# Seven half-size block products in place of eight in the first projection of a squared-ReLU MLP, from the second chunk on

## The reference, cut to what matters

```python
x = x + y
x = x + squared_relu_mlp(rms_norm(x, mlp_norm[i]), mlp_w1[i], mlp_w2[i])
```

## Time and profile before

| what | value |
| --- | --- |
| median of 3 runs | 2267.03 us (2266.93 to 2268.66) |
| the profiled execution | 2264.53 us |
| its span in the profile | 2262.7 us (1.8 us lie around it) |
| TensorE busy | 2093.1 us, 93% of the span |
| VectorE, ScalarE, GpSimd busy | 1262.4, 968.8 and 260.1 us |
| the MLP | about 1594 to 2259 us of the span |

### The profile page before, as it was taken

The page is one execution under the profiler, slowest core; times in us unless marked ns, Lnnn a source line. Parts: engine busy times, 40 slices in busy tenths (PEclk is TensorE's granted clock), DMA queues, the critical chain, the costliest instruction groups (busy, mean ns, idle before and its releaser), DMA issues. The chain is left out here.

```text
span 2262.7 us, 28831 instructions
## 1 busy us (share of the span) xinstructions
PE 2093.1 (93%) x11131; PEld 1095.9 (48%) x11131; DVE 1262.4 (56%) x1346; ACT 968.8 (43%) x1256; POOL 260.1 (11%) x263
## 2 busy tenths in 40 slices
PE   7988988889499999999958999969899999999999
PEld 5445446644354454454435665624444444444444
DVE  5134237743799999999976352555443333433432
ACT  5122226722388888888845342452311211211210
POOL 0000130000133333333200000050000000000000
PEclk9999999999699999999979999989999999999999
DMA  6111220051399999999984352342220111111101
GB/s 265 38 38 38 71 51 1 1 217 47 109 416 412 412 404 410 399 400 404 367 310 156 104 187 62 92 126 108 75 75 37 38 73 37 62 49 37 37 0 75
DMA packets 74718, 352.98 MB, mean 156 GB/s; under 512 B 16336, under 2 KB 23120, under 8 KB 42064
## 3 DMA queue, kind: packets, MB, share of 16 engines
q1 hardware_dynamic: 56304, 305.21, 34.7%
q0 software_dynamic: 18336, 46.69, 6.3%
HBM read 326.67 MB, written 29.36 MB: 157 GB/s over the span
## 5 line engine op out<-in xcount | busy, mean ns | idle before, releaser
L409 PE MATMUL ps<-xt,split 128*128 128x512 f16 (+1 forms) x1024 | 377.8, 369 | 10.0 <-issue 8.3
L410 PE MATMUL ps<-xt,split 128*128 128x512 f16 (+1 forms) x1024 | 378.0, 369 | 0.0
L411 PE MATMUL ps<-xt,split 128*128 128x512 f16 (+1 forms) x1024 | 377.9, 369 | 0.0
L409 PE MATMUL ps<-split,xt 128*128 128x512 f16 x928 | 354.0, 381 | 25.5 <-DMA xt<-arena 19.5
L410 PE MATMUL ps<-split,xt 128*128 128x512 f16 x928 | 353.9, 381 | 0.0
L411 PE MATMUL ps<-split,xt 128*128 128x512 f16 x928 | 353.6, 381 | 0.0
L540 DVE SCALAR_TENSOR_TENSOR split<-stage,split 128x2048 f16<-128x2048 f32 x128 | 289.4, 2282 | 5.6 <-ACT split L536 3.9
L536 ACT ACTIVATE split<-stage 128x2048 f16<-128x2048 f32 x128 | 240.5, 1904 | 94.2 <-PE ps L411 94.2
L1773 DVE SCALAR_TENSOR_TENSOR resid<-ps,resid 128x512 f32<-128x512 f32 x128 | 87.1, 690 | 191.7 <-PE ps L411 191.6
L409 PE MATMUL ps<-split,arena 128*128 128x512 f16 x512 | 194.0, 379 | 0.0
L410 PE MATMUL ps<-split,arena 128*128 128x512 f16 x512 | 194.0, 379 | 0.0
(11 more groups left out here) (293 smaller groups left out, 3149.4 us busy)
## 6 DMA issues: line engine op xcount, KB each, us to landing
stage<-in_w_gate SPq DMA_DIRECT2D x64, 1024.0 KB, 7.4
stage<-in_w_up SPq DMA_DIRECT2D x64, 1024.0 KB, 7.7
arena<-in_w_down SPq DMA_DIRECT2D x64, 1024.0 KB, 8.3
stage<-in_w_mlp SPq DMA_DIRECT2D x32, 1024.0 KB, 5.0
arena<-in_conv_taps POOLq DMA_DIRECT2D x32, 576.0 KB, 4.2
stage<-in_w_dense_a SPq DMA_DIRECT2D x16, 1024.0 KB, 7.7
stage<-in_w_dense_b SPq DMA_DIRECT2D x12, 1024.0 KB, 9.6
resid<-in_x SPq DMA_DIRECT2D x16, 512.0 KB, 4.8
```

The costliest lines, as they stand in the source:

```text
L409: nc.tensor.matmul(out_ap, lh, rh, start=start, stop=False)
L410: nc.tensor.matmul(out_ap, lh, rl, start=False, stop=False)
L411: return nc.tensor.matmul(out_ap, ll, rh, start=False, stop=stop)
```

## The change

It replaces the first projection of chunks 1 to 7. A chunk's w1 is cut into four quarters, A11, A21 (slot 0) and A12, A22 (slot 1); the first index is the half of the features, the second the half of the inputs in the order that the loads bring them. The input is cut into four blocks by input half and token half. Eight products of a quarter with a block become seven (Strassen's scheme in the form with S1 to S4 on the weight side, T1 to T4 on the input side).

- **TensorE:** seven products (`PRODUCTS`), each two groups (f = 0 into `PS`, f = 1 into `PT`) of 4 pieces x 3 = 12 matmuls of 512 columns.
- **GpSimd:** in each chunk, four sums of 128x1024 float32 in place in `stage` (S1, S3, S2, S4), after the low part of A22 has been made.
- **ScalarE, VectorE:** seven operands of 128x1024 are split (`op_hi`, `op_lo`) instead of two units of 128x2048.
- **Once, in chunk 0:** VectorE makes T1 to T4, in two parts each, from `XT2` (`combo_of`, 20 operations of 128x1024, every one with two operands in SBUF), then their low parts (`combo_lo`, 8); ScalarE makes the high parts (`combo_hi`, 8). T1 comes in the second projection of chunk 0.
- **VectorE, in each chunk from 1 on:** 14 sums of products (`bank_sum`, 128x512), 8 relu-times-itself (`quad_relu`) and 8 low parts (`quad_lo`); ScalarE 2 copies and 8 high parts.
- **SP:** slots 0 and 1 are reloaded once all seven operands of the chunk have been split (`s_pl`).
- w1 is laid out by quarters in DRAM. A few semaphores of earlier stages are shared; their counts are raised to match.

```diff
         def mlp_chunks(eng, body):
-            with eng.Fori(0, NC - 1) as c:
+            with eng.Fori(1, NC - 1) as c:
                 body(c, False)
             body(NC - 1, True)
...
+        OP_AT = {"A11": split[:, 0:2048], "A12": split[:, 2048:4096], "S4": split[:, 4096:6144],
+                 "A22": split[:, 6144:8192], "S2": Z[:, 0:1024].bitcast(F16), "S3": junk[:, :].bitcast(F16),
+                 "S1": Z[:, 1280:2304].bitcast(F16)}
...
+        PRODUCTS = ["A11", "A12", "S2", "S3", "A22", "S1", "S4"]
...
+        FACTOR = {"A11": "B11", "A12": "B21", "S4": "B22", "A22": "T4", "S1": "T1", "S2": "T2", "S3": "T3"}
+        COMBOS = [("T3", 0), ("T3", 1), ("T2", 0), ("T2", 1), ("T4", 0), ("T4", 1), ("T1", 0), ("T1", 1)]
...
                 for s in range(SLOTS):
-                    sp.wait_ge(s_wh[s], RM + c)
-                    sp.wait_ge(s_wo[s], RM + c)
+                    if s < 2 and not (isinstance(c, int) and c < 2):
+                        sp.wait_ge(s_pl, 7 * (c - 1))
+                    else:
+                        sp.wait_ge(s_wh[s], RM + c)
+                        sp.wait_ge(s_wo[s], RM + c)
...
+            with pool.Fori(1, NC) as c:
+                for s in range(2):
+                    pool.wait_ge(s_wl[s], 16 * (RM + 1) + 16 * c)
+                pool.wait_ge(s_pl, 7 * (c - 1) + OP_N["A22"])
+                nc.gpsimd.tensor_tensor(quarter(1, 1), quarter(0, 1), quarter(1, 1), ALU.add).then_inc(s_sm, 1)
+                pool.wait_ge(s_sm, 4 * (c - 1) + 1)
...
+                if name == "T3":
+                    ch.done(nc.vector.tensor_tensor(t, part(4, r + 2, 0), part(0, r + 2, 0), ALU.subtract))
+                    ch.done(nc.vector.tensor_tensor(t, t, part(4, r + 2, 1), ALU.add))
+                    i = nc.vector.tensor_tensor(t, t, part(0, r + 2, 1), ALU.subtract)
...
+            for j in range(8, 24):
+                down_sum(j, G_MLP + j // 4 + 1)
+                if j in (8, 9, 10):
+                    op_lo(dve, ("A11", "A12", "A22")[j - 8], 1)
+                if j in (11, 13):
+                    combo_of("T1", (j - 11) // 2)
+                if j in (15, 16):
+                    combo_lo("T1", j - 15)
+                if j in (17, 19, 20, 21):
+                    op_lo(dve, {17: "S2", 19: "S3", 20: "S1", 21: "S4"}[j], 1)
...
+                def bank_sum(out, f, n, v):
+                    dve.wait_ge(s_uf, 14 * (c - 1) + 2 * n + f + 1)
+                    nc.vector.tensor_tensor(out[f], (PS, PT)[f][:, n % 4, :], v[f], ALU.add).then_inc(s_ud, 1)
...
+                for f in range(2):
+                    bank_sum(U_X, f, 5, U_X)
+                for f in range(2):
+                    bank_sum(U_V, f, 5, U_V)
+                for f in range(2):
+                    summed(4, f)
+                    quad_relu(2, f)
+                for f in range(2):
+                    quad_lo(2, f)
+                for f in range(2):
+                    summed(5, f)
+                    bank_sum(U_V, f, 6, U_V)
+                for f in range(2):
+                    summed(6, f)
+                    quad_relu(3, f)
+                for f in range(2):
+                    quad_lo(3, f)
+                if not last:
+                    op_lo(dve, "A22", c + 1)
                 for j in range(8, 24):
...
+                    down_sum(j, G_DOWN + 4 * (c - 1) + j // 4 - 1)
+                    if not last and j in (13, 15, 17, 19):
+                        op_lo(dve, {13: "S2", 15: "S3", 17: "S1", 19: "S4"}[j], c + 1)
...
+                    for kk in range(UK):
+                        cs = slice(kk * HF + f * P, kk * HF + f * P + P)
+                        i = product(pe, (PS, PT)[f][:, n % 4, :], w[:, 0:1024][:, cs], w[:, 1024:2048][:, cs],
+                                    x[:, kk, :, 0:MC], x[:, kk, :, MC:2 * MC], kk == 0, kk == UK - 1)
+                    i.then_inc(s_uf, 1)
```

More of the change, by code:

```diff
@@ L274, in build @@
         s_gain = sem("gain_loaded")
-        s_x = [sem(f"x_loaded{i}") for i in range(TT)]
+        s_x = [sem(f"rows_loaded{i}") for i in range(TT)]
         s_wl = [sem(f"w_landed{i}") for i in range(6)]
@@ L338, in build @@
         s_ys = [sem(f"y_stored{i}") for i in range(2)]
-        s_yg = [sem(f"y_gathered{i}") for i in range(4)]
         s_cmb = sem("combined")
@@ new lines, in build, with quad_at @@
+        HALVES = [(0, 0), (2, 0), (2, 1), (0, 1)]
+        UP = [[AR[:, 4096 + 512 * i:4608 + 512 * i] for i in range(2)], [AR[:, 5120 + 512 * i:5632 + 512 * i]
+              for i in range(2)], [xn[:, 0, 512 * i:512 * i + 512] for i in range(2)],
+              [xn[:, 1, 512 * i:512 * i + 512] for i in range(2)]]
+        U_V, U_X, U_Y, U_W = UP
+        QUADS = [U_W, U_Y, U_X, U_V]
+        def quad_at(v, q, f):
+            k0, t = HALVES[q]
+            return v[:, k0 + f, 512 * t:512 * t + 512]
@@ new lines, in _ @@
+            for j in range(9):
+                if j < 8:
+                    act.wait_ge(s_full[j % 4], G_MLP + j // 4 + 1)
+                    if j >= 2:
+                        act.wait_ge(s_ml, j - 1)
+                    nc.scalar.activation(relu[j % 2], PS[:, j % 4, :], ACT.Relu, scale=IWS).then_inc(s_free[j % 4], 1)
+                if j:
+                    h = j - 1
+                    act.wait_ge(s_free[h % 4], G_MLP + h // 4 + 1)
+                    nc.scalar.activation(HTh[:, h % 4, (h // 4) * 512:(h // 4) * 512 + 512], relu[h % 2],
+                                         ACT.Square).then_inc(s_mh, 1)
+                if 1 <= j <= 6:
+                    combo_hi(act, *COMBOS[j - 1])
@@ new lines, in _, with down_units @@
+            for name in ("A11", "A12", "A22"):
+                op_hi(act, name, 1)
+            for r in range(2):
+                combo_hi(act, "T1", r)
+            for name in ("S2", "S3", "S1", "S4"):
+                op_hi(act, name, 1)
+            def down_units(c):
+                for s in (2, 3):
+                    act.wait_ge(s_full[3], G_DOWN + 4 * c)
+                    act.wait_ge(s_full[2], G_DOWN + 4 * c)
+                    mlp_hi(act, s, c + 1)
+            down_units(0)
@@ new lines, in body, with copied, quad_hi @@
+            def body(c, last):
+                def copied(f):
+                    act.wait_ge(s_uf, 14 * (c - 1) + f + 1)
+                    act.wait_ge(s_ml, 8 * c)
+                    nc.scalar.activation(U_V[f], (PS, PT)[f][:, 0, :], ACT.Copy).then_inc(s_ua, 1)
+                def quad_hi(q, f):
+                    act.wait_ge(s_relu, 8 * c + 2 * q + f + 1)
+                    nc.scalar.activation(quad_at(HTh, q, f), QUADS[q][f], ACT.Copy, scale=IWS * IWS).then_inc(s_mh, 1)
+                for f in range(2):
+                    copied(f)
+                for f in range(2):
+                    quad_hi(0, f)
+                if not last:
+                    op_hi(act, "A11", c + 1)
+                    op_hi(act, "A12", c + 1)
+                for q in range(1, 4):
+                    for f in range(2):
+                        quad_hi(q, f)
+                if not last:
+                    for name in ("A22", "S2", "S3", "S1", "S4"):
+                        op_hi(act, name, c + 1)
+                    down_units(c)
@@ new lines, in combo_of @@
+            def combo_of(name, r):
+                t = combo(r)
+                if name == "T3":
+                    ch.done(nc.vector.tensor_tensor(t, part(4, r + 2, 0), part(0, r + 2, 0), ALU.subtract))
+                    ch.done(nc.vector.tensor_tensor(t, t, part(4, r + 2, 1), ALU.add))
+                    i = nc.vector.tensor_tensor(t, t, part(0, r + 2, 1), ALU.subtract)
+                elif name == "T2":
+                    ch.done(nc.vector.tensor_tensor(t, t, part(0, r, 0), ALU.add))
+                    i = nc.vector.tensor_tensor(t, t, part(0, r, 1), ALU.add)
+                elif name == "T4":
+                    ch.done(nc.vector.tensor_tensor(t, part(4, r, 0), t, ALU.subtract))
+                    i = nc.vector.tensor_tensor(t, t, part(4, r, 1), ALU.add)
+                else:
+                    ch.done(nc.vector.tensor_tensor(t, part(0, r + 2, 0), part(0, r, 0), ALU.subtract))
+                    ch.done(nc.vector.tensor_tensor(t, t, part(0, r + 2, 1), ALU.add))
+                    i = nc.vector.tensor_tensor(t, t, part(0, r, 1), ALU.subtract)
+                i.then_inc(s_cmb, 1)
@@ new lines, in combo_lo, with down_sum @@
+            def combo_lo(name, r):
+                n = COMBOS.index((name, r)) + 1
+                dve.wait_ge(s_xh, 5 * TT + n)
+                nc.vector.tensor_tensor(XT_OP[name][:, :, r, MC:2 * MC], combo(r), XT_OP[name][:, :, r, 0:MC],
+                                        ALU.subtract).then_inc(s_xl, 1)
+                dve.wait_ge(s_xl, 5 * TT + n)
+            def down_sum(j, n):
+                t, hs = (j - 8) // 2, slice(j % 2 * 512, j % 2 * 512 + 512)
+                dve.wait_ge(s_full[j % 4], n)
```

(45 more changed lines are left out.)

205 lines of the change are left out of this document (131 added, 74 removed).

## The result

The changed kernel takes 2230.97 us (median of 4 runs, 2229.15 to 2234.07) against 2267.85 us before (2266.93 to 2269.11): a ratio of 0.9838, 95% interval 0.9821 to 0.9855. The forecast was 2232.7 us, the range 2229.5 to 2241. The profiled execution has a span of 2228.6 us.

What follows compares the result with a forecast made beforehand. TensorE was taken to bound the MLP, at 0.2158 us a matmul. Removed matmuls -36.3 us and a chunk 0 loss of +1.9 give -34.4, against the median 2267.03: 2232.7 us, range 2229.5 to 2241.

Steps and rivals of the forecast that it cites:

- main term: First projections of chunks 1 to 7: 168 matmuls fewer at 0.2158 us each, saving 36.3 us.
- loss of 1.9 us: Chunk 0, second projection: GpSimd sums and T1 operations take turns, delaying the j = 14 bank; 1.9 us lost.
- 4g + 6 x 1.27: Chunk 0: four GpSimd sums of g us each (g taken as 2.3) and six T1 operations follow each other.
- cover in the later chunks: After E, the first projection's end: VectorE frees bank 0 2.7 us before TensorE wants it for j = 12; no cost.
- rival 3: VectorE's queue is late in every chunk, waits costing 0.2 us more an operation: 2247 us; chance 0.08.
- 1.3 us that I kept for a drop: Chunk 0: added cost if the clock drops once, beside a 5.4 us loss: 2237.5 us in all; chance 0.1.
- Rival 4: GpSimd sums have a large fixed part, 1024 columns taking as long as 2048: slower, 2290 us; chance 0.04.
- 4g - 16.2: Loss in each of six later chunks if GpSimd sums of g us hold up S2's low part; nothing up to 4.05.

Runs made afterwards that it cites:

- eight fillers: Changed kernel with eight added VectorE operations of 0.72 us per chunk from 1 on, between the last sums of products and the last relu: 2236.88 us, ratio 0.9865.
- tripled sums: Changed kernel with two more GpSimd operations of 128x1024 on a free tile before each of the four sums: 2244.25 us, ratio 0.9892.
- twelve fillers: Changed kernel with twelve added VectorE operations per chunk from 1 on, 8.7 us in all, before the last relu: 2271.95 us, ratio 1.0014.

## Why the prediction was right

**The main term.** 168 x 0.2158 = 36.3 us: the stretch shrank by 35.8 and lost 0.5 to a pause. Computing one product twice brings the time of before back (ratio 0.9999, 0.0010 either way) and the stretch to 621.5 us. Shown.

**Chunk 0.** The place (the bank of j = 14, wanted for j = 18), the cause (T1 beside the sums) and the sum's own time (2.3 forecast, 2.35 measured) were right; the loss of 1.9 us was 0.5. The term "4g + 6 x 1.27" was mis-sized: I let every pair cost g plus a whole operation of VectorE, 3.6 us, and it costs 3.28. Of VectorE's 1.23 us some 0.9 exclude GpSimd. From the start of the sums to the end of T1 the term gives 16.8 us, and the rows 15.8 (1648.70 to 1664.53). The sums also began 0.2 us earlier than I had put it, at E + 9.9, and from T1's end to TensorE's start it took 0.65 us and not 0.9. Together these are the 1.4 us of difference. Moving the sums behind T1 took away the long operations and the pause, so the cause is shown.

The rule of the Trainium skill that I drew on (SBUF — State Buffer, Who interferes with whom: the one that comes later is blocked for the whole length of the other) holds as to who waits for whom in this stretch, also for VectorE's bank sums, which have only one operand in SBUF and one in PSUM. Two of them stand in the midst of the fourth GpSimd sum, at 1658.63, and all 128 took 0.68 to 0.69 us:

```profile
L1901 DVE SCALAR_TENSOR_TENSOR resid<-ps,resid x128: 675/692/692, 1642.8 to 2224.8; 128x512 f32<-128x512 f32 x128
```

The price of a meeting is lower than that of the two operations in a row, 3.28 instead of 3.58 us, and the measurement decides. The estimate of 2.25 us for a sum of 1024, half of what the Trainium skill gives for 2048 (GPSIMD Engine Reference, 3.1 Elementwise — side-by-side cycle accounting), is 0.1 below the rows.

One row of the kernel before doesn't fit, and I had not used it. Beside the second TENSOR_SCALAR of the earlier trace rows, which lasts from 331.61 to 337.95, VectorE does this:

```profile
334.33 2.02 DVE L1501 SCALAR_TENSOR_TENSOR xt<-xt,cols 128x128 f32<-128x128 f32 x1
```

It has two operands in SBUF and was held, since the shortest execution of L1501 takes 0.35 us, but it was done 1.6 us before GpSimd. So that VectorE waits for the whole of the other operation is shown for TENSOR_TENSOR on GpSimd; for TENSOR_SCALAR this row speaks against it, and why stays open.

**The cover in the later chunks.** Forecast 2.7 us, measured some 4.7 by the trace and 4.7 to 4.8 by eight fillers. The step was "20 operations of 512 columns at 0.69": two that don't depend on each other start 0.60 us apart. It cost the forecast nothing, since both covers are positive, but it made rival 3 likelier than it was: at 0.2 us more an operation it would still have lost nothing in the later chunks.

**Clock.** That pauses of about 1 us leave it alone was right (0.3, 0.9 and 1.7 us). The 1.3 us that I kept for a drop are the lower end: after pauses of 2.4 us and more it was 1.3 to 2.9.

**Rival 4.** The formula 4g - 16.2 lets all four GpSimd sums go ahead of the low part of S2. The tripled sums bear the reason out: that low part has to wait for ScalarE's high part (1.06 us), by then GpSimd's next operation is under way, and VectorE ends 1.1 us after it. In that run the next operation was a short added one; in the changed kernel it is the fourth sum. What was off is the start: the sums begin at E + 5.0 and not at E + 7.6. With 0.08 us between sums, 1.07 us from the end of the fourth to the end of the low part, and 0.65 us from there to TensorE, a single sum could last some 4.7 us, an estimate, before the first loss in those chunks. I had put that at 4.05. No run made the sums themselves longer, so the 4.7 is not shown.

**The median.** Between 2232.7 and 2230.97 lie 1.7 us. Chunk 0 is 1.4 of them. The rest is within the spread of the stages ahead of the MLP; the medians of the kernel before differ too, from 2267.03 to 2269.06 over the sets of runs. The measured difference of 36.9 us is 1.1 more than the 35.8 of the stretch, by the same spread.

## What to carry to other kernels

When one engine is busy without a gap, price a change first by that engine's instructions, counted between two far-apart rows, and then ask of each other engine only by when its result is wanted; a queue with 45 of 78 us of work was no risk, and the one place with a pause was the one where one-time work and recurring work met in the same stretch. Test such a reading by putting the removed work back and leaving the added work in. Look at the trace of an experiment even if its time agrees: twelve fillers gave the forecast +41 us with two errors that cancelled.

## What the runs showed of the hardware that I had not expected

- Pauses of TensorE of 0.3, 0.9 and 1.7 us were followed by matmuls 0.22 us apart. Pauses of 2.4, 2.5, 3.0 and 3.8 us were followed by 7 to 14 matmuls 0.43 us apart, in two cases after two or four that were still 0.22 us apart. A pause of 3.8 us thus cost up to 6.8.
- A VectorE operation of 1024 columns with two operands in SBUF and a GpSimd sum of 1024, alone 1.23 and 2.35 us, took 3.28 us as a pair, in turn, for as long as both had work.
- A GpSimd TENSOR_TENSOR of 128x1024 float32 whose three operands are one and the same tile took 1.89 us, the sums over different tiles 2.35:

```profile
1650.03 1.89 POOL L1185 TENSOR_TENSOR gb<-gb 128x1024 f32<-128x1024 f32 x1 [126.20 <-DVE split L708]
```
